# A two-layer HGRN2 and mLSTM step: packed matmuls for scores and gates, sums by block, added-up tiles for mean and variance

## The reference, cut to what matters

```python
def rmsnorm(x, g):
    y = x32 * lax.rsqrt(jnp.mean(x32 * x32, axis=-1, keepdims=True) + EPS)
...
# HGRN2, in each chunk: decayed scores, output, new state
    A = jnp.einsum('bhtk,bhsk,bhtsk->bhts', qc, kc, decay)
    o = jnp.einsum('bhtk,bhkv->bhtv', qc * jnp.exp(b), S) + jnp.einsum('bhts,bhsv->bhtv', A, vc)
...
# mLSTM: gates from q, k and v, then the scan, then a norm over each head
    ig = (gin @ p['ml_wig'][j] + p['ml_big'][j]).astype(F32)
    lf = jax.nn.log_sigmoid((gin @ p['ml_wfg'][j] + p['ml_bfg'][j]).astype(F32))
...
    mu = jnp.mean(hc, axis=-1, keepdims=True)
    var = jnp.mean((hc - mu) ** 2, axis=-1, keepdims=True)
...
# trunk, for each layer
    mod = cmod @ p['w_ada'][l] + p['b_ada'][l]
    h = rmsnorm(x, p['norm_g'][l, 0]) * (1 + sc1) + sh1
    x = x + g1 * mix
    x = x + g2 * hier_moe(...)
```

## Time and profile before

| | |
|---|---|
| Median of 3 runs | 2088.66 us (2088.17 to 2096.98) |
| The profiled execution | 2091.45 us, its span 2089.9 us |
| Mean granted TensorE clock | 0.923 of full speed |
| Instructions | 24152 |
| Read from HBM, written | 275.49 MB, 70.03 MB (165 GB/s over the span) |

### The profile page before, as it was taken

How to read it: one execution, slowest core, us unless ns; L and a number is a source line. 1 busy time by engine, 2 the same in 40 slices (tenths; PEclk the granted TensorE clock), 3 DMA queues, 4 the chain that set the end, 5 groups by cost and what they waited for, 6 DMA issues and landing times.

```text
span 2089.9 us, 24152 instructions
## 1 busy us (share of the span) xinstructions
PE 1846.5 (88%) x9666; PEld 1356.6 (65%) x9666; DVE 750.7 (36%) x1632; ACT 412.1 (20%) x641; POOL 180.8 (9%) x274
## 2 busy tenths in 40 slices
PE   5999999997979996899979899999999997987983
PEld 2777777765758884676644654646546775875863
DVE  1244344443142112454564444453553004211114
ACT  3222233331031111311131120311201003011111
POOL 0000000000011111000003012020030001021100
PEclk9999999997979998899989999999999997888995
DMA  8334444453138997211117218054082212668913
GB/s 332 137 137 142 142 142 140 140 190 117 62 107 274 336 315 264 95 41 40 51 45 274 109 59 303 21 212 160 25 299 86 70 62 83 226 239 315 320 72 136
DMA packets 93986, 330.18 MB, mean 158 GB/s; under 512 B 15504, under 2 KB 15504, under 8 KB 93120
## 3 DMA queue, kind: packets, MB, share of 16 engines
q1 hardware_dynamic: 63648, 234.13, 32.3%
q0 software_dynamic: 30240, 94.67, 12.2%
HBM read 275.49 MB, written 70.03 MB: 165 GB/s over the span
## 4 chain that ended last, share of the span: by engine, by line
PE 73%; DVE 12%; DMA 7%; ACT 3%; issue 3%; POOL 1%; DVEq 0%; POOLq 0%; SPq 0%; ACTq 0%
PE ps L558 28%; PE ps L853 11%; PE ps L859 5%; PE ps L659 4%; PE ps L570 3%; DMA arena<-h_rows,idx 2%; PE ps L580 2%; PE ps L1139 2%; PE ps L676 2%; PE ps L865 2%; DMA out_mc_s<-ring 2%; DMA ring<-in_c 1%; PE ps L1112 1%; PE ps L617 1%; PE ps L1095 1%
## 5 line engine op out<-in xcount | busy, mean ns | idle before, releaser
L558 PE MATMUL ps<-hT,ring 128*128 128x288 f32 x1792 | 467.5, 423 | 35.6 <-ACT hT L1204 11.2
L558 PEld LDWEIGHTS ps<-hT,ring 128*128 128x128 f32 x1792 | 353.7, 199 | 143.0 <-DVE xT L2104 14.0
L853 PEld LDWEIGHTS ps<-arena,ring 128*128 128x128 f32 x2048 | 244.2, 199 | 21.1 <-issue 14.4
L853 PE MATMUL ps<-arena,ring 128*128 128x128 f32 x2048 | 245.3, 283 | 6.6 <-DVE arena L1789 5.3
L558 PE MATMUL ps<-arena,ring 128*128 128x288 f32 x768 | 191.0, 413 | 3.8 <-DVE arena L2171 3.8
L558 PEld LDWEIGHTS ps<-arena,ring 128*128 128x128 f32 x768 | 148.5, 194 | 45.9 <-DVE arena L2171 4.2
L1796 DVE TENSOR_TENSOR arena<-ps,arena 128x128 f32<-128x128 f32 x64 | 18.6, 291 | 288.7 <-ACT arena L1310 288.7
L859 PE MATMUL ps<-ring,arena 128*128 128x512 f32 x256 | 115.9, 597 | 0.0
L659 PE MATMUL ps<-ring,hT 128*128 128x128 f32 (+1 forms) x640 | 77.9, 284 | 1.0 <-DVE arena L1632 1.0
L659 PEld LDWEIGHTS ps<-ring,hT 128*128 128x128 f32 (+1 forms) x640 | 76.2, 191 | 2.9 <-DVE arena L1632 1.9
L859 PEld LDWEIGHTS ps<-ring,arena 128*128 128x128 f32 x256 | 46.9, 193 | 47.5 <-issue 47.5
(11 more groups left out here) (405 smaller groups left out, 2313.8 us busy)
## 6 DMA issues: line engine op xcount, KB each, us to landing
ring<-in_wstream SPq DMA_DIRECT2D x376, 512.0 KB, 5.1
ring<-in_c SPq DMA_DIRECT2D x32, 512.0 KB, 6.7
arena<-in_c SPq DMA_DIRECT2D x32, 512.0 KB, 6.8
out_mc_s<-arena POOLq DMA_DIRECT2D x64, 256.0 KB, 5.3
out_mc_s<-ring POOLq DMA_DIRECT2D x64, 256.0 KB, 6.5
arena<-y_rows POOLq DMA_DIRECT2D x8, 1024.0 KB, 8.3
arena<-in_hg POOLq DMA_DIRECT2D x8, 512.0 KB, 4.0
out_hg_s<-arena POOLq DMA_DIRECT2D x8, 512.0 KB, 2.9
```

The source lines that it names most:

```text
L558: mm = pe.matmul(ps[:, 2 * p + half, 0:TH], ring[:, r, c * P:(c + 1) * P], rhs(k)[:, TH * half:TH * (half + 1)], start=(k == 0), stop=(k = ...
L853: mm = pe.matmul(ps[:, n // 2, P * (n % 2):P * (n % 2 + 1)], w[:, P * c:P * (c + 1)], rows[:, c, :], start=(c == 0), stop=(c == DC - 1))
```

## The change

- **First loads.** `ada_first` is cut in two: steps 0 and 1 run ahead of the sums of the first norm, steps 2 and 3 behind them. No DMA instruction is changed.
- **Scores.** The 32 queries are the weights now and the decayed keys move (128 columns); the four blocks of a chunk write to four groups of 32 partitions. ScalarE copies the result to a new tile `A`, TensorE transposes it ahead of the scan, and VectorE's mask moves behind `Vx`.
- **Sample states.** Each of the two update matmuls of `scan` takes only the 32 rows that can be other than zero in its half.
- **Sums by block.** In the combining, block j-1 is summed right after the transposes of block j, the last one after the loop.
- **Gates.** The weights have 32 columns. Five matmuls for each tile write to four groups of partitions: by kind of input and by half of the tokens. After the last tile VectorE copies the bank, two matmuls with a selecting matrix `sel` add the groups, and VectorE reads the gates before it makes the first head's weights.
- **Mean and variance.** VectorE adds the four tiles, and later the four squared tiles, into `mx["mu"]`; TensorE sums one tile each time.
- Three semaphores get a second use (`turned_s`, `dn_read`, `dn_full`), counted on from H.

```diff
@@ start
-            norm_sums(0)
-            ada_first()
+            pe.wait_ge(s["silc"].sem, 1)
+            pe.wait_ge(pair_free[0].sem, USES["ada"] // 2)
+            ada_first((0, 1))
+            norm_sums(0)
+            ada_first((2, 3))
@@ sums by block
+            def block_sums(n, j):
+                m = P if j < 4 else 64
+                pe.wait_ge(s["sq_ready"].sem, SQ_AT[n] + j + 1)
+                dst = ps[:, 6, P * j:P * (j + 1)] if j < 4 else ps[:, 7, 0:64]
+                for c in range(DC):
+                    mm = pe.matmul(dst, ones, hT[:, c, P * j:P * j + m], start=(c == 0), stop=(c == DC - 1))
+                if j == TJ - 1:
+                    s["ss_ready"].on(mm)
@@ scores
-                        pe.matmul(ps[:, 4, at:at + BLK], hg["K"][:, 4 * c + i, :], hg["eq"][:, at:at + BLK],
-                                  start=True, stop=True)
+                        mm = pe.matmul(ps[BLK * i:BLK * (i + 1), 4, c * P:(c + 1) * P], hg["eq"][:, at:at + BLK],
+                                       hg["K"][:, 4 * c + i, :], start=True, stop=True)
+                s["raw_scores"].on(mm)
@@ scan
+                pe.wait_ge(s["raw_read"].sem, h + 1)
+                for c in range(4):
+                    mm = pe.transpose(ps[:, 4, c * P:(c + 1) * P], hg["A"][:, c, :], ident)
+                s["scores_turned"].on(mm)
                 pe.wait_ge(pair_free[1].sem, 3 * h + (uh + 3))
-                pe.wait_ge(s["at_ready"].sem, 2 * h + 2)
+                pe.wait_ge(s["at_ready"].sem, 2 * h + 1)
...
                 pe.wait_ge(s["vx_ready"].sem, h + 1)
+                pe.wait_ge(s["at_ready"].sem, 2 * h + 2)
                 for half in range(2):
-                    mm = pe.matmul(ps[:, 4 + 2 * half, :], hg["ktw"][0:64, 4, :],
-                                   hg["Vx"].rearrange("p a b -> p (a b)")[0:64, 512 * half:512 * (half + 1)],
+                    of_half = slice(BLK * half, BLK * (half + 1))
+                    mm = pe.matmul(ps[:, 4 + 2 * half, :], hg["ktw"][of_half, 4, :],
+                                   hg["Vx"].rearrange("p a b -> p (a b)")[of_half, 512 * half:512 * (half + 1)],
@@ combining
                     s["comb_full"].on(mm)
+                    if j:
+                        block_sums(2 * layer + 2, j - 1)
+                block_sums(2 * layer + 2, TJ - 1)
@@ gates
-                pe.matmul(ps[0:64, 6, 0:TP], gm, first["xpad"][:, u, 3:3 + TP], start=start, stop=False)
-                pe.matmul(ps[0:64, 6, 0:TP], gx, xc_i[:, 0:TP], start=False, stop=stop)
-                pe.matmul(ps[0:64, 7, 0:64], gm, first["xs"][:, u, :], start=start, stop=False)
-                s["gates_full"].on(pe.matmul(ps[0:64, 7, 0:64], gx, xc_i[:, TP:T], start=False, stop=stop))
+                xp, xs = first["xpad"][:, u, 3:3 + TP], first["xs"][:, u, :]
+                dst = [ps[32 * g:32 * (g + 1), 6, 0:TH] for g in range(4)]
+                pe.matmul(dst[0], gm, xp[:, 0:TH], start=start, stop=stop)
+                pe.matmul(dst[2], gx, xc_i[:, 0:TH], start=start, stop=stop)
+                pe.matmul(dst[1][:, 0:TP - TH], gm, xp[:, TH:TP], start=start, stop=stop)
+                pe.matmul(dst[3], gx, xc_i[:, TH:T], start=start, stop=stop)
+                s["gates_full"].on(pe.matmul(dst[1][:, TP - TH:TH], gm, xs, start=False, stop=stop, skip_group_check=True))
+
+            def gate_sums():
+                pe.wait_ge(s["gates_read"].sem, 1)
+                parts, sel = ml["W"][:, 0, 0:TH], first["sel"]
+                pe.matmul(ps[0:64, 7, 0:TH], sel[:, 0, :], parts, start=True, stop=True)
+                s["gates_full"].on(pe.matmul(ps[0:64, 5, 0:TH], sel[:, 1, :], parts, start=True, stop=True))
@@ end of an mLSTM head, TensorE
-                pe.wait_ge(pair_free[(hb + 21) % 2].sem, (hb + 21) // 2 + 1)
                 p = use()
-                s["mu_full"].on(wide((2 * p, 2 * p + 1), [ones] * HT, [ml["q"][:, i, :] for i in range(HT)]))
+                pe.wait_ge(s["hsum_ready"].sem, 2 * h + 1)
+                s["mu_full"].on(wide((2 * p, 2 * p + 1), [ones], [mx["mu"]]))
                 gate_tile(h, 2)
-                pe.wait_ge(s["sqh_ready"].sem, h + 1)
                 p = use()
-                s["var_full"].on(wide((2 * p, 2 * p + 1), [ones] * HT, [sqh[:, i, :] for i in range(HT)]))
+                pe.wait_ge(s["hsum_ready"].sem, 2 * h + 2)
+                s["var_full"].on(wide((2 * p, 2 * p + 1), [ones], [mx["mu"]]))
@@ ScalarE, in evict, ahead of the copies of the values
+                if scored:
+                    raw_scores(h - 1)
@@ VectorE, in scan, behind Vx
+                dve.wait_ge(s["scores_turned"].sem, h + 1)
+                s["at_ready"].on(tt(hg["at"][:, 0:4, :], shaped(ps[:, 4, :], 4, P),
+                                    causal.unsqueeze(1).broadcast_to([P, 4, P]), ALU.mult))
@@ VectorE, in an mLSTM head
+                    if i:
+                        dve.wait_ge(pair_free[p].sem, n // 2 + 1)
+                        ins = tt(mx["mu"], ml["q"][:, 0, :] if i == 1 else mx["mu"], ml["q"][:, i, :], ALU.add)
+                        (V if i < HT - 1 else s["hsum_ready"]).link(dve, ins)
...
+                for i in range(1, HT):
+                    ins = tt(mx["mu"], sqh[:, 0, :] if i == 1 else mx["mu"], sqh[:, i, :], ALU.add)
+                    (V if i < HT - 1 else s["hsum_ready"]).link(dve, ins)
```

More of the change, by code:

```diff
@@ L249, in build @@
             ("qe", T), ("kw", T), ("at", TJ, P), ("ktw", TJ, P), ("S", 4, P), ("sq", T),
-            ("rs", T), ("Sn", NB, P), ("half", H), ("low", H), ("t1", 3, H), ("t2", H),
+            ("rs", T), ("Sn", NB, P), ("A", 4, P), ("half", H), ("low", H), ("t1", 3, H), ("t2", H),
             ("keep", T)])
@@ L584, in ada_step, with ada_first @@
                             used.on(mm)
-            def ada_first():
-                pe.wait_ge(s["silc"].sem, 1)
-                pe.wait_ge(pair_free[0].sem, USES["ada"] // 2)
-                for si in range(4):
+            def ada_first(steps):
+                for si in steps:
                     ns = [RING["ada"] + 4 * si + j for j in range(4)]
@@ L602, in turn_ada_rows @@
                 s["turned"].on(mm)
-            def norm_sums(n):
-                if n in (2, 4):
-                    for j in range(TJ):
-                        m = P if j < 4 else 64
-                        pe.wait_ge(s["sq_ready"].sem, SQ_AT[n] + j + 1)
-                        dst = ps[:, 6, P * j:P * (j + 1)] if j < 4 else ps[:, 7, 0:64]
-                        for c in range(DC):
-                            mm = pe.matmul(dst, ones, hT[:, c, P * j:P * j + m], start=(c == 0), stop=(c == DC - 1))
-                    s["ss_ready"].on(mm)
-                    return
+            def block_sums(n, j):
[6 more added lines that the diff above has]
+                    s["ss_ready"].on(mm)
+            def norm_sums(n):
                 for c in range(DC):
@@ L725, in _ @@
             mod_step(0, 0, 1)
-            per = {used: 24, s["scored"]: 2, s["scored_s"]: 2, s["upd"]: 2, s["upd_s"]: 2, s["o_full"]: 4,
+            per = {used: 24, s["raw_scores"]: 2, s["scores_turned"]: 2, s["scored"]: 2, s["scored_s"]: 2, s["upd"]: 2, s["upd_s"]: 2, s["o_full"]: 4,
                    s["head_ss"]: 2}
@@ L978, in _ @@
                 gates(j, 7, False, j == 1)
+            gate_sums()
             ub = USES["b"]
@@ L1107, in prompt_state @@
                     if k == 0:
-                        pe.wait_ge(s["dn_read"].sem, h + 1)
+                        pe.wait_ge(s["dn_read"].sem, H + h + 1)
                     else:
@@ L1158, in _ @@
             moe(1)
-            norm_sums(4)
         def halves(p):
@@ L1228, in _, with raw_scores, evict @@
             base = RING["hg"]
-            def evict(u, h, guarded):
+            def raw_scores(h):
+                act.wait_ge(s["raw_scores"].sem, h + 1)
+                s["raw_read"].on(act.copy(hg["A"].rearrange("p c n -> p (c n)"), ps[:, 4, :]))
+            def evict(u, h, guarded, scored=True):
                 if guarded:
@@ L1261, in head_norm @@
                 s["head_rs"].on(act.activation(hg["rs"], hg["rs"], ACT.Exp, scale=-0.5))
-            evict(0, 0, False)
+            evict(0, 0, False, False)
             exponentials(0)
@@ L1275, in _ @@
             exponentials(H - 1)
+            raw_scores(H - 1)
             head_norm(H - 1)
@@ L1921, in _ @@
             V.link(dve, dve.memset(first["gm"], 0.0))
+            V.link(dve, dve.memset(first["sel"], 0.0))
+            for half in range(2):
+                for kind in range(2):
+                    at_g = 32 * half + 4 * kind
+                    V.link(dve, tt(first["sel"][:, half, 32 * kind:32 * kind + 4], ident[:, at_g:at_g + 4],
+                                   ident[:, 64 + at_g:64 + at_g + 4], ALU.add))
             V.link(dve, dve.memset(first["xpad"][:, :, 0:3], 0.0))
@@ L1994, in _ @@
             dve.wait_ge(s["gates_full"].sem, MT)
```

(12 more changed lines are left out.)

25 lines of the change are left out of this document (13 added, 12 removed).

## The result

| | median us | lowest to highest | runs |
|---|---|---|---|
| before | 2088.41 | 2086.25 to 2096.98 | 4 |
| after | 2019.99 | 2018.12 to 2023.98 | 4 |

The ratio is 0.9677, 95% interval [0.966, 0.9694]. The forecast was 2020 us (2002 to 2042), faster with a chance of 0.97. The sum came out right. Its terms did not: two were too small and two too large. The profiled execution of the kernel after has a span of 2019.3 us, 70.6 less than before.

A forecast was written before the change was run, and what follows sets the result against it. The prediction took TensorE, busy 88% of the span, as the bound. Terms 3.6 + 21 + 8 + 18 + 19.2 = 69.8 us off 2091.45 gave 2021.7, or 2018.9 by the median; forecast 2020 us, range 2002 to 2042.

The forecast's parts named there:

- Start: First loads and first norm: first row copied at 37.3 instead of 40.94, gain 3.6 us (bounds 0 and 6.1).
- Scores: Eight HGRN2 heads, packed scores and sample update: 17.2 us in seven heads, 21 us with the last (bounds -14 and 27).
- Gain 2.1 us: HGRN2 scores per head: 32 packed records at 0.047 us take 1.5 us instead of 3.59.
- Sums by block: Combining, both layers: sums between transposes gain 4 us each, 8 in all; 9 to 9.6 if they raise the clock.
- Gates: mLSTM gates, 16 tiles: 0.82 us instead of 2.04, gain 1.22 x 15; term 18 us (bounds -6 and 22).
- Net 0.3 lost: End of the gates: new chain of copy, two matmuls and four copies, against 2.3 us saved on the last tile.
- Mean and variance: Four mLSTM heads: 4 records replace 16 each time, 4.8 us a head, 19.2 us (bounds 8 and 21).
- The lower clock: Rival, 2036 us, chance 0.13: short gaps slow tiles behind the mean to 1.2 GHz; block sums gain nothing.
- A loss at changes of tile shape: Rival, 2031 us, chance 0.07: 24 sets, two switches each at up to 0.2 us, drain the array, 9.6 us.
- Packed records overlap throughout: Opposes two rivals: short packed sets do not overlap, 2076 us, chance 0.05; each record waits for the last, 2147, 0.02.

The follow-up runs named there:

- The kernel before with wide scores: Kernel before, each HGRN2 score matmul moving all 128 queries, not 32, against the old weights; 2019.43 us, not comparable because expert tiles differ; HGRN2 stage 13.7 us shorter.
- The partial sums aside: Kernel after, gate sums copied to another buffer so VectorE makes the first head's weights while TensorE adds the partial sums; 2018.51 us, one run.
- three moves of order: Kernel after with keys by token moved into TensorE's wait, spread values before the next head's rows, and gate sums copied aside, all at once; 1985.16 us, ratio 0.9503.
- without the wait: Kernel after with VectorE making the spread values Vx before the next head's rows: 2003.46 us, ratio 0.9594; the same order combined with two other moves: 1985.16 us.
- scores of 32 columns: Kernel after with packed HGRN2 scores cut to 32 of 128 moving columns, outputs differing; only the stage is read, ending 10.6 us earlier than in the kernel after.

## Why the forecast was right, and which terms were not

**Start (3.6, measured 4.8).** Two misses of opposite sign. The half-modulation ran at the pace of its slots, but to 24.43 and not to 22.5 (22.5 and 10.97 make 33.5, too, not the 33.7 of the sum). And I had priced the sums behind it at their present 10.97 us; they took 8.03, the price of 32 such records at 2.4 GHz, which I had kept for the upper bound.

**Scores (21, measured 28 to 32 by place, 29.6 by time).** The step "Gain 2.1 us" a head took four-group records at 0.047 us each from L1039. They cost 0.031 (0.99 us for 32). The 0.047 was a misreading: it is busy time over four sets of 16 records, of which the first ran at a granted clock of 0.50 (1.01 us from its start to the next work), and the other three took 0.57, which is 0.036 a record. The first two sets in the profile of before, each with the work behind it:

```profile
1072.17 1.08 PE L1039 MATMUL ps<-arena 128*32 128x128 f32 x16
1073.19 5.73 PE L1044 MATMUL ps<-arena 128*128 128x128 f32 x32
...
1208.34 0.64 PE L1039 MATMUL ps<-arena 128*32 128x128 f32 x16
1208.91 3.84 PE L1044 MATMUL ps<-arena 128*128 128x128 f32 x32
```

The seven plain heads gain 2.7 from the scores, lose 0.49 to the transposes, and gain 0.74 at the update and its wait: 2.97 each, 20.8 together against the 17.2 of the forecast. The step that was missing is the clock: behind the old scores four of seven value groups, and the last head, ran partly at 1.2 GHz. The kernel before with wide scores shows it: 13.7 us for work that is no shorter. The forecast had a lower clock in the last head only, 3.8 us; the last head gained 9.3 and the values 4.1, and cold scans took some of it back. No run undoes the row groups of the sample update alone; its 0.74 is read from the rows.

**Sums by block (8, measured 7 to 8 by place, 2.5 by time).** The Ln came 2.75 us behind the last block, not 8.3. As forecast, the first block's sums ran at the lower clock (3.68 us) and made VectorE late once, by 1.15 us; the next took 1.95. I had read the granted clock of 0.59 as half of the time at 1.2 GHz; with two levels, 0.5 and 1, it is about four fifths. The Trainium skill ("TensorE: Matmul & The Clock Gate", Part 4) says that a transpose does not count as busy in the way that a matmul does, and from that I had inferred that the sums would raise the clock. The trace agrees with the inference: eight records of transposes took 1.97 us ahead of the first sums and 1.04 behind them. It doesn't show that the kind of work is the reason, for TensorE is also busy for more of the stretch, 13.84 of 16.9 us against 7.68 of 13.6. The term did not come to 9. Why the time shows less than the place is open: the difference lies in stages that the edit does not touch.

**Gates (18, measured 16.3 by place, 10.2 by time).** A tile's gates take 0.62 us, not 2.04, and a tile is 1.33 us shorter, against 1.22 forecast. Two things stand against it. The last tile of each of the two rounds of eight waits for ScalarE's activation of the convolved channels (2.98 us idle ahead of L981), as it did before (3.81 us ahead of L966), and there the shorter gates save almost nothing: of 19.9 us only 17.9 arrive. And the tail, from the last gates to the first queries, went from 5.56 to 7.69 us, 2.1 where "Net 0.3 lost" stood: the two matmuls take 2.2 us with their hand-overs (990.73 to 992.95) at a granted clock of 0.50, and the weights are made last. The partial sums aside shows that 3.3 of the 7.69 were order alone.

**Mean and variance (19.2, worth 20.5 by time).** At their places they gain 2.94 and 2.84 us, less 0.96 before and 0.55 between, 4.3 a head and 17.1 in all. Against the profile of before the heads came out only 8.2 shorter, which looked like a failed term. Undoing the part, and running the kernel after again, showed that it was not: the heads hold small losses of clock that fall elsewhere in other executions. The last six query tiles of head 1 (24 records) took 7.82 us in the first profile of the kernel after and 6.15 in the second.

**Rivals.** The lower clock is real, and it moved. Behind the scores of the HGRN2 heads it went away; in the scans it came in with the change, which has two or three cold ones in each profile with the wait of 1.22 us, where no profile with the old scores has one that is cold throughout (2.27 us at most). Over the heads as a whole the granted clock is 0.94 before (74.5 to 502 us) and 0.95 and 0.94 in the two profiles of the kernel after. A loss at changes of tile shape isn't seen: a set of 32 packed records between full-width neighbours cost 0.99 us with both of its changes, less than the 1.5 that the sum had for it without any. Whether a tenth or two of the 0.99 go to such a loss, the rows don't show. Packed records overlap throughout.

The sum was right partly by luck: 7 to 11 us too little in the scores, 2 to 3 too much in the gates, and 3 to 11 too much in the heads of the one profile I compare with.

## What to carry to other kernels

Price a stretch together with what runs behind it: 3.7 us of scores bound by weight loads cost up to 1.6 us more in the full-width matmuls that followed. Before a part is judged by a stage of one profile, look at how far untouched stages move between executions (here up to 7 us, and 8 for the same kernel); undo the part and time it. Where a change adds a small chain between two stages, look what each engine does while it waits in it: three moves of order, without any new arithmetic, were worth half as much as the whole change.

## What the runs showed of the hardware

- Packed fp32 matmuls with 32-column weights in four groups cost 0.031 us a record at 128 moving columns and 0.015 at 32 (0.48 us for 32 records), though a record's own length is 273 and 203 ns.
- With 128-column weights, 32 or 128 moving columns cost nearly the same, 3.76 and 3.84 us for 32 records, but in the third head the granted clock of the next 10 us was 0.85 and 1.00. With 32 columns the values behind were slowed in four of seven heads in each of two profiles, with 128 in none of one profile.
- A wait of 1.22 us behind the values, with whole packed scores, went with two or three scans at the lower clock in each of seven profiles; without the wait, or with scores of 32 columns, there were none in three profiles.
- The same kernel had granted clocks of 0.91 and 0.95 over 500 us of its mLSTM heads in two executions whose times differ by 3 us: 7 us less of TensorE's busy time in that stage, mostly given back in others.
